# A MoE block's expert loop regrouped: steps of four experts with 32 slots each, in place of two with 64

## The reference, cut to what matters

```python
def hier_moe(xn, w_rg, b_rg, w_re, b_re, w_gu, w_dn):
    pg_top, g_top = lax.top_k(pg, 1)
...
    pe_top, e_top = lax.top_k(jax.nn.softmax(le_sel, axis=-1), TOP_K_IN_GROUP)
...
    for gi in range(N_GROUPS):
        gate, up = jnp.split(jnp.einsum('nd,edf->nef', t, w_gu[gi]), 2, axis=-1)
        hmid = jax.nn.silu(gate) * up * comb[:, gi, :, None].astype(t.dtype)
        out = out + jnp.einsum('nef,efd->nd', hmid, w_dn[gi])
```

## Time and profile before

| | |
|---|---|
| median of 3 runs | 616.98 us (614.00 to 617.87) |
| profiled execution, span from the first to the last instruction | 615.0 us |
| TensorE busy, share of the span | 533.6 us, 87% |
| VectorE, ScalarE, GpSimd | 195.9, 130.9, 45.4 us |
| DMA traffic | 134.37 MB, 218 GB/s over the span |

### The profile page before, as it was taken

One profiled execution on the slowest core, in us unless ns is written; L12 is line 12 of the kernel. 1 busy time (PEld: TensorE's weight loads), 2 busy tenths in 40 slices (PEclk: granted clock), 3 DMA queues, 4 the chain that ended last, 5 costly groups with the idle time before them and its releaser, 6 DMA issues.

```text
span 615.0 us, 7497 instructions
## 1 busy us (share of the span) xinstructions
PE 533.6 (87%) x2783; PEld 328.0 (53%) x2783; DVE 195.9 (32%) x577; ACT 130.9 (21%) x275; POOL 45.4 (7%) x84
## 2 busy tenths in 40 slices
PE   0799999999996999997699999999999999999700
PEld 0665545665665677664674455555555455555200
DVE  1100001243535345354651223332332223332236
ACT  5312012111111535244111111111111111111003
POOL 4000021000004010010000000000000000000000
PEclk9879999999996799898599999999999999999865
DMA  8994251000019312004329999999999999994053
GB/s 273 386 386 75 93 195 45 2 0 1 0 37 416 146 34 77 11 2 175 135 101 355 378 376 376 403 392 372 374 373 379 374 383 377 382 377 150 10 189 130
DMA packets 35793, 134.37 MB, mean 218 GB/s; under 512 B 11250, under 2 KB 11286, under 8 KB 31672
## 3 DMA queue, kind: packets, MB, share of 16 engines
q1 hardware_dynamic: 32280, 127.17, 55.0%
q0 software_dynamic: 2912, 4.77, 2.1%
q10 hardware_dynamic: 576, 2.10, 0.9%
HBM read 127.68 MB, written 11.58 MB: 226 GB/s over the span
## 4 chain that ended last, share of the span: by engine, by line
PE 85%; DVE 6%; ACT 3%; DMA 3%; issue 2%; SPq 0%; POOLq 0%; DVEq 0%; ACTq 0%
PE bank L1294 81%; DMA X<-in_x 1%; ACT V L837 1%; DMA r_xs<-pair_rows 1%; PE bank L1482 1%; DVE X L1274 1%; PE bank L1401 1%; PE bank L1323 1%; DMA pair_rows<-r_xs,sidx_now 1%; DVE X L1282 1%; DVE r_xs L920 1%; DVE pnorm L980 0%; ACT r_xT L681 0%; PE bank L1452 0%; DVE r_qz L1066 0%
## 5 line engine op out<-in xcount | busy, mean ns | idle before, releaser
L1294 PE MATMUL bank<-gu_ring,r_xT 128*64 128x512 f32 (+1 forms) x560 | 133.9, 592 | 0.0
L1294 PEld LDWEIGHTS bank<-BT,r_qz 128*128 128x128 f32 x768 | 88.8, 195 | 14.7 <-issue 14.2
L1294 PE MATMUL bank<-BT,r_qz 128*128 128x128 f32 x768 | 91.8, 280 | 3.1 <-DVE BT L1168 2.8
L1294 PEld LDWEIGHTS bank<-gu_ring,r_xT 128*64 128x64 f32 (+1 forms) x560 | 50.6, 142 | 79.1 <-issue 76.9
L1294 PE MATMUL bank<-dn_ring,V 128*64 128x512 f32 x256 | 59.6, 607 | 12.8 <-ACT V L837 12.8
L1294 PE MATMUL bank<-r_xT,gu_ring 128*128 128x384 f32 x192 | 65.3, 501 | 0.0
L1294 PEld LDWEIGHTS bank<-r_xT,gu_ring 128*128 128x128 f32 x192 | 37.5, 197 | 25.5 <-issue 2.3
L1294 PE MATMUL bank<-r_xT,dn_ring 128*128 128x384 f32 x128 | 42.6, 486 | 0.0
L1294 PEld LDWEIGHTS bank<-dn_ring,V 128*64 128x64 f32 x256 | 18.5, 139 | 43.8 <-issue 34.1
L1229 DVE COPY r_xs<-bank 128x512 f32<-128x512 f32 x16 | 11.1, 692 | 84.5 <-PE bank L1294 84.5
L816 ACT ACTIVATE r_xT<-bank 128x512 f32<-128x512 f32 x32 | 19.1, 598 | 81.6 <-PE bank L1294 81.6
(11 more groups left out here) (244 smaller groups left out, 505.4 us busy)
## 6 DMA issues: line engine op xcount, KB each, us to landing
gu_ring<-in_w_expert_gate_up SPq DMA_DIRECT2D x32, 2048.0 KB, 8.7
dn_ring<-in_w_expert_down SPq DMA_DIRECT2D x32, 1024.0 KB, 8.6
gu_ring<-in_w_in SPq DMA_DIRECT2D x4, 2048.0 KB, 14.2
dn_ring<-in_w_in SPq DMA_DIRECT2D x2, 2048.0 KB, 18.5
gu_ring<-in_w_out SPq DMA_DIRECT2D x2, 2048.0 KB, 9.2
r_xs<-in_cache_k SPq DMA_DIRECT2D x8, 256.0 KB, 8.9
r_xs<-in_cache_v SPq DMA_DIRECT2D x8, 256.0 KB, 6.6
r_xs<-pair_rows SPq DMA_DIRECT2D x4, 512.0 KB, 5.1
```

Source lines behind the costliest of these rows:

```text
L1294: return te.matmul(out, lhsT, rhs, start=start, stop=stop, **kw)
```

## The change

`SLOTS` becomes 32, and a step takes four experts (`WIDE` = 4, `QUADS` = 8 steps): gate-up and down write to four groups of 32 rows of a bank, from four column groups of 32 columns. All four slots of the ring now belong to one step. The gate-up load of an expert is cut in two halves of 1.05 MB (slices 0 to 3 and 4 to 7 of D), each with semaphores of its own; `gate_up` waits for the four first halves, runs its first half, signals `gu_mid`, waits for the second halves, and signals `gu_full` at its end. Loads of step n + 1 are issued after `gu_mid(n)`, `gu_full(n)` and `y_full(n)`. The overflow table has 12 columns of counts in place of 6 and is built after step 0; the counts are copied out of their bank ahead of `pick_step(0)`. All steps are written out. The overflow loop stays as it was, with 32 slots; pairs of rank 32 and above now go there, which for these inputs is one block (the 4 last pairs of expert 1).

```diff
-SLOTS = 64
+SLOTS = 32
+WIDE = 4
...
-DUOS = E // 2
+QUADS = E // WIDE
+HALF_K = KT // 2
...
+            def load_up(n, h, half):
+
+                ks = slice(half * HALF_K * 2 * F, (half + 1) * HALF_K * 2 * F)
+                sp.dma_start(gu_ring[:, h, ks], w_gu[n * WIDE + h][:, ks]).then_inc(ld_gu[half][h], 16)
+
+            def load_down(n, h):
+                sp.dma_start(dn_ring[:, h, :].rearrange("p (j n) -> p j n", j=FT), w_dn[n * WIDE + h]).then_inc(ld_dn[h], 16)
...
-            with sp.Fori(1, E // RING) as i:
-                for u in range(2):
-
-                    sp.wait_ge(gu_full, i * 2 + (u - 1))
-                    for r in (2 * u, 2 * u + 1):
-                        sp.dma_start(gu_ring[:, r, :], w_gu[i * RING + r]).then_inc(ld_gu[r], 16)
-                    sp.wait_ge(y_full, i * 2 + (u - 1))
-                    for r in (2 * u, 2 * u + 1):
-                        sp.dma_start(dn_ring[:, r, :].rearrange("p (j n) -> p j n", j=FT), w_dn[i * RING + r]).then_inc(ld_dn[r], 16)
+            for half in range(2):
+                for h in (0, 1):
+                    load_up(0, h, half)
+            for n in range(1, QUADS):
+                sp.wait_ge(gu_mid, n)
+                for h in range(WIDE):
+                    load_up(n, h, 0)
+                sp.wait_ge(gu_full, n)
+                for h in range(WIDE):
+                    load_up(n, h, 1)
+                sp.wait_ge(y_full, n)
+                for h in range(WIDE):
+                    load_down(n, h)
...
             dve.wait_ge(rk_full, 1)
+            dve.wait_ge(cnt_full, 1)
             link(v.tensor_copy(rk[:, :, :], bT[0][:, 0:TT * E].rearrange("p (t e) -> p t e", t=TT)))
...
+            link(v.tensor_copy(cnt[:, :], bS[0][:, 0:E]))
...
-                for k in range(KT):
-                    if k % 4 == 0:
-                        pe.wait_ge(xgt_evac, n * 2 + (k // 4 + 1))
-                    for h in range(2):
-                        rows = slice(h * SLOTS, (h + 1) * SLOTS)
-                        ins = mm(bG[buf][rows, :], xgT[buf][:, k, rows], gu_ring[:, 2 * buf + h, k * 2 * F:(k + 1) * 2 * F], k == 0, k == KT - 1)
-                ins.then_inc(gu_full, 1)
...
+                for half in range(2):
+                    pe.wait_ge(xgt_evac, n * 2 + (half + 1))
+                    for h in range(WIDE):
+                        pe.wait_ge(ld_gu[half][h], n * 16 + 16)
+                    for k in range(half * HALF_K, (half + 1) * HALF_K):
+                        for h in range(WIDE):
+                            rows = slice(h * SLOTS, (h + 1) * SLOTS)
+                            ins = mm(bG[n % 2][rows, :], xgT[n % 2][:, k, rows], gu_ring[:, h, k * 2 * F:(k + 1) * 2 * F], k == 0, k == KT - 1)
+                    ins.then_inc(gu_full if half else gu_mid, 1)
...
             def down(n):
                 pe.wait_ge(ht_evac, n + 1)
-                for r in (2 * buf, 2 * buf + 1):
-                    pe.wait_ge(ld_dn[r], turn * 16 + 16)
+                for h in range(WIDE):
+                    pe.wait_ge(ld_dn[h], n * 16 + 16)
```

More of the change, by code:

```diff
@@ L314, in build @@
         st_krow = [sem(f"st_krow{i}") for i in range(2)]
-        ld_gu = [sem(f"ld_gu{i}") for i in range(RING)]
+        ld_gu = [[sem(f"ld_gu{half}{i}") for i in range(RING)] for half in range(2)]
         ld_dn = [sem(f"ld_dn{i}") for i in range(RING)]
@@ L615, in _, with step @@
             pool.wait_ge(sca_done, 1)
[L617 to L621, removed]
+            def step(n):
+                u = n % 2
+                if n >= 2:
+                    pool.wait_ge(scattered[u], n // 2 * 16)
+                g.tensor_copy(sidx_now[u][:, :], sca_i[:, n:n + 1]).then_inc(sidx_set, 1)
                 pool.wait_ge(sidx_set, n + 1)
@@ L629, in step @@
                                         bounds_check=PAIRS - 1, oob_is_err=False).then_inc(scattered[u], 16)
[L631 to L637, removed]
+            for n in range(QUADS):
+                step(n)
+            pool.wait_ge(scattered[0], QUADS // 2 * 16)
+            pool.wait_ge(scattered[1], QUADS // 2 * 16)
+            pool.wait_ge(ovr_regs, 1)
             n_ov = pool.value_load(ov_regs[0:1, 2 * OVROWS:2 * OVROWS + 1], min_val=0, max_val=MAXOV)
@@ L838, in step @@
                 act.wait_ge(y_half, n + 1)
[L839 to L854, removed]
+                if n >= 2:
+                    act.wait_ge(scattered[n % 2], n // 2 * 16)
+                s.activation(y_rows[n % 2][:, 0:512], bO[0][:, :], ACT.Copy).then_inc(y_evac_a, 1)
+                if n + 1 < QUADS:
+                    gate_exp(n + 1)
+            rows_evac(0)
+            gate_exp(0)
+            for n in range(QUADS):
+                step(n)
+            act.wait_ge(ovr_regs, 1)
             n_ov = act.value_load(ov_regs[0:1, 2 * OVROWS:2 * OVROWS + 1], min_val=0, max_val=MAXOV)
@@ L1159, in pick_step @@
                     dve.wait_ge(key_c, n)
-                if not first:
+                if n >= 2:
                     dve.wait_ge(xgt_full, n * 2 - 2)
@@ L1541, in hidden_transpose @@
-            def hidden_transpose(n, buf, first):
+                for half in range(2):
+                    pe.wait_ge(xgt_evac, n * 2 + (half + 1))
[6 more added lines that the diff above has]
+                    ins.then_inc(gu_full if half else gu_mid, 1)
@@ L1550, in down @@
                 pe.wait_ge(ht_evac, n + 1)
[L1551 to L1552 removed]
+                for h in range(WIDE):
+                    pe.wait_ge(ld_dn[h], n * 16 + 16)
                 for half, evac, done in ((0, y_evac_a, y_half), (1, y_evac_d, y_full)):
[L1554 removed]
+                    if n >= 1:
                         pe.wait_ge(evac, n)
                     for j in range(FT):
[L1558 removed]
+                        for h in range(WIDE):
@@ L1575, in _ @@
             pe.wait_ge(xn2_scaled, TT)
-            pick_rows(0, 0, 0, KT, True)
+            pick_rows(0)
             pe.wait_ge(key_done, 1)
-            for half in range(2):
-                rows = slice(half * SLOTS, (half + 1) * SLOTS)
+            for h in range(WIDE):
+                rows = slice(h * SLOTS, (h + 1) * SLOTS)
                 for j in range(2 * TT):
-                    ins = mm(bS[1][rows, 0:DUOS], ranked[:, j // TT, j % TT, :], oh[:, j // TT, j % TT, half::2], j == 0, j == 2 * TT - 1)
+                    ins = mm(bS[1][rows, 0:QUADS], ranked[:, j // TT, j % TT, :], oh[:, j // TT, j % TT, h::WIDE], j == 0, j == 2 * TT - 1)
@@ L1601, in _ @@
+            for n in range(1, QUADS):
+                step(n)
+            pe.wait_ge(y_evac_a, QUADS)
+            pe.wait_ge(y_evac_d, QUADS)
+            pe.wait_ge(ovr_regs, 1)
             n_ov = pe.value_load(ov_regs[0:1, 2 * OVROWS:2 * OVROWS + 1], min_val=0, max_val=MAXOV)
```

205 lines of the change are left out of this document (93 added, 112 removed).

## The result

The changed kernel takes 619.54 us (median of 20 runs, 613.48 to 621.22), the kernel before, timed beside it, 616.46 (20 runs, 611.55 to 617.98). The ratio is 1.0041, interval [1.0025, 1.0058]: 0.4% slower, where 0.5% faster was forecast. The profiled execution has a span of 618.2 us; the sum had given 611.9.

The account below looks back on a forecast made before the run. TensorE was taken to bound the old steps, loads ending just inside. Last load 543.0, plus 5.3 last down, 39.6 overflow block and 24.0 unchanged, gave span 611.9; with the profile-to-median difference, 614 us, range 600 to 628.

Parts of the forecast that it names:

- the sum: Whole kernel: predicted stage times added up to the row reload at 587.9, plus 24.0 us unchanged: span 611.9 us.
- TensorE in a step of four: Four-expert steps: TensorE work lies between 17.1 and 27.8 us a step, depending on column groups; 18 taken.
- Loads of a step of four: Four-expert steps: loads run without a gap and set the pace, 32.2 us a step, bounds 30.2 and 34.2.
- the loads run free: Rival, steps: down loads and scatter don't hurt each other, 30.2 us a step, 600 us in all; chance 0.20.
- down at 345 GB/s: Steps: down loads run at this rate with a scatter beside them, 12.2 us a step; 10.2 at 410.
- The cover of 12 us: Steps: each load is issued with 12 us or more to spare before the queue runs dry.
- Start: Ahead of the steps: picks start at 303.3, gate-up at 312.6, and the first load goes out at 316.1.
- last down: End of the steps: `down(7)` takes 5.3 us after the last load lands at 543.0, ending at 548.3.
- The overflow block: Behind the last step: new work with nothing beside it, 39.6 us to the reload, costing 33.2 us extra.
- TensorE stays at half clock in the overflow block: Rival, behind the steps: search, numbers, gate-up and both downs doubled, block costs 45 us, 628 in all; chance 0.14.
- steps paced as today: Rival, steps: loads keep 379 GB/s, 34.2 us a step, 628 us in all; chance 0.12.
- half clock and TensorE: Two rivals: overflow block at half clock, 628 us, chance 0.14; TensorE binding the steps, 648 us, chance 0.05.

Follow-up runs that it names:

- the early table: The changed kernel with the overflow table built before VectorE's wait for `y_full` of step 0; 618.02 us, ratio 1.0023 to the kernel before.
- the filler run: The changed kernel with 16 unused matmuls of 512 columns between the last step and the overflow block; 614.48 us, ratio 0.9971 to the kernel before.
- the hoisted block: The changed kernel, overflow table made early, first block's base, picks and slot numbers between steps 6 and 7, its loads issued earlier; 593.74 us.

## Why the prediction was wrong

The direction was wrong, by 5.5 us in time. The range held, but by luck: it was drawn for the rate of the loads and for the clock, and the largest miss is a wait for which it had no term. By its own steps:

*TensorE in a step of four* was right: all four column groups run at once. At full clock the matmuls of a step are 16.9 us (picks 5.6, transposes 0.4, down 3.6, gate-up 7.2, from 364 to 381), with 18 taken; in the steps that wait for loads, part of it runs at half clock and TensorE is busy for 20 of 31 us (77.8 of 120 from 380 to 500). *Loads of a step of four* went to the rival: 31.0 us a step in place of 32.2, near the 30.2 of "the loads run free". The term that was mis-sized is down at 345 GB/s. It was read from windows in which the loads waited for TensorE, and the kernel before with fewer picks shows the same traffic at 400. The gain didn't all arrive: at 1.2 us for each of seven steps the last load should have landed 8.4 us ahead of the 543.0 of the sum, and it came 2.3 ahead. The sum had no term for the end of the queue, where the rate falls from 406 to 111 GB/s (about 3 us by the windows), nor for the dip (1.7 us by its bytes). *The cover of 12 us* held in all steps but at the table, where it was used up: the 7.9 us of wait there, and the picks behind it at part half clock (7.5 us in place of 5.6), let the down loads of step 2 go out at 368.06, against 356.85 with the early table, and the rate dips from 365 to 375. What the dip costs in the end isn't shown; the run without it was 0.6 us shorter, inside the spread. *Start* and *last down* were right: picks at 302.99 (303.3), first load at 316.11 (316.1), 5.34 us (5.3). Together these put the end of the last down at 546.0, 2.3 us ahead of the predicted 548.3. That this is so near is in part luck, since the better rate and the missing end of the queue had opposite signs.

*The overflow block* is the step that failed. From the end of down(7) to the reload it takes 48.1 us, predicted 39.6. Stage by stage against the sum:

| stage | predicted | measured |
|---|---|---|
| scatter landed | 5.3 | 11.4 (546.0 to 557.35) |
| GpSimd and VectorE set up | 2.8 | 3.0 |
| TensorE finds the rows | 7.5 | 10.4 |
| slot numbers | 1.3 | 0.7 |
| gate-up | 6.9 | 8.8 |
| SiLU | 3.5 | 3.5 |
| transposes and copy | 1.15 | 0.8 |
| down | 4.8 | 5.3 |
| copies, scatter, signal | 6.35 | 4.3 |
| sum | 39.6 | 48.1 |

The largest miss, 6.1 us, is the scatter. The prediction took the 3.57 us of the earlier trace rows, where nothing else flew. It said that the block's weights "land under the search of rows", and never asked what these loads do to the scatter that the block waits for. With the loads behind the scatter the wait falls from 8.78 to 2.34 us. The price could have been read from the trace of the kernel before. This is its row for the scatters, with the median us from issue to landing:

```profile
pair_rows<-r_xs,sidx_now POOLq DMA_INDIRECT x16, 8.0
```

The 14 scatters that had loads beside them took 7.5 to 9.2 us there, and only the last two, with an empty queue, 2.6 and 3.6. The prediction took one of these two, which were not like its case. The next two, 2.9 and 1.9 us, are half clock in search and gate-up, which the sum had mostly at full clock: the rival "TensorE stays at half clock in the overflow block" was right on these, though its price for them was larger. With a warm clock the search lost 3.75 us; that gate-up would lose its 1.9 too was not shown by that run, but where gate-up follows the last down without a gap it does take 7.03.

In sum: -2.3 for the steps, +8.5 for the block, +0.1 behind it, 6.3 us over the predicted span. The two errors had opposite signs, so the time alone makes both look smaller than they are. Inside the block, too, the last row took 2.05 us less than in the sum: its scatter had nothing beside it (2.40 us).

The part that outweighs every term is one that the prediction took as given: that the block stands behind the steps. Nothing lies beside it there, and it costs 42 us; among the steps it costs 9. The chance given to "slower" came from steps paced as today, half clock and TensorE, and none from a longer wait inside the block.

## What to carry to other kernels

When a change gives a rare case a path of its own, price that path where it stands: four pairs of tokens undid all that the wider steps had won, and the same work laid into the steps' idle time kept three quarters of it. Read a transfer rate only where nobody makes the queue wait; a share of 0.98 at 379 GB/s was still demand. Ask of each load that is issued early what small transfer on a chain it now runs beside.

## What the runs showed of the hardware

- A small indirect scatter of 128 rows lands 2.3 to 3.7 us after its issue ends when it is alone (loads behind the scatter 2.34, kernel before 2.6, without the block 3.74), and 8.8 when two loads of 2.1 and 1.05 MB are issued within a microsecond of it. The steps of the kernel before show the same: 7.5 to 9.2 us from issue to landing beside loads. There no chain waits for it, so it costs nothing.
- The share of the DMA engines' time was 0.98 at 379 GB/s in the steps before, 1.00 at 400 with fewer picks, and 1.01 at 414 after: a share near 1 didn't say how much more could be moved.
- The clock fell from 1.00 to 0.52 while TensorE was busy without a break, in matmuls of 32 columns (the filler run, 558 to 564), after 14 us of wide ones; it came back within the gate-up that followed. In the hoisted block the same 48 records ran at 1.00 to their end, and it fell just behind them. What makes it fall there isn't shown.
- Four column groups of 32 give nearly the full fourfold in float32: 0.115 us for a record of 512 columns, against 0.44 us where a single group runs alone (7.03 us for the 16 records of the block's gate-up).
